# Squares turned and totalled by VectorE, masks added by VectorE, spreads a chunk or more later, gates kept in PSUM, and a launch from a feature-major copy of the input

## The reference

```python
x = x + 0.5 * swiglu(rms_norm(x, g1), w_gate, w_up, w_down)   # width 2816
x = x + mixing(rms_norm(x, g2), ...)
x = x + 0.5 * swiglu(rms_norm(x, g3), ...)
```

## Time and profile before

| | |
|---|---|
| median of 3 runs | 2061.31 us (2059.57 to 2062.02) |
| the profiled execution | 2060.95 us, of which the span from first to last instruction is 2059.0 us |
| TensorE, matmuls | 2031.1 us busy (99% of the span) |
| TensorE, weight loads | 1755.1 us (85%) |
| VectorE | 805.0 us (39%) |
| ScalarE | 1082.1 us (53%) |
| GpSimd | 1575.6 us (77%) |
| transfers | 362.29 MB, 176 GB/s on average |

### The profile page before, as it was taken

The page is one execution under the profiler, slowest core; times in us unless marked ns, Lnnn a source line. Parts: engine busy times, 40 slices in busy tenths (PEclk is TensorE's granted clock), DMA queues, the critical chain, the costliest instruction groups (busy, mean ns, idle before and its releaser), DMA issues.

```text
span 2059.0 us, 35031 instructions
## 1 busy us (share of the span) xinstructions
PE 2031.1 (99%) x12172; PEld 1755.1 (85%) x12172; DVE 805.0 (39%) x1776; ACT 1082.1 (53%) x1879; POOL 1575.6 (77%) x672
## 2 busy tenths in 40 slices
PE   8999999999999999999999999999999999999998
PEld 7888988888888898888888888888888888878887
DVE  3223744222422374422242237632223224763223
ACT  5445545444555554544455457654455445755444
POOL 6888756888888875688888886378887887546886
PEclk9999999999999999999999999999999999999999
DMA  7555534555555553455555554455555555444553
GB/s 251 191 187 184 185 114 130 188 191 186 179 187 192 178 185 113 133 191 186 191 177 188 189 188 135 159 177 188 190 188 180 186 191 177 145 177 156 189 192 125
DMA packets 100977, 362.29 MB, mean 176 GB/s; under 512 B 11808, under 2 KB 13088, under 8 KB 100768
## 3 DMA queue, kind: packets, MB, share of 16 engines
q1 hardware_dynamic: 100320, 359.78, 52.5%
q10 hardware_dynamic: 576, 1.41, 0.2%
HBM read 360.10 MB, written 1.05 MB: 175 GB/s over the span
## 4 chain that ended last, share of the span: by engine, by line
PE 94%; DVE 3%; ACT 1%; DMA 1%; issue 1%; SPq 0%; POOLq 0%; DVEq 0%; POOL 0%; ACTq 0%
PE twin L623 30%; PE twin L629 19%; PE twin L697 9%; PE twin L699 9%; PE twin L698 9%; PE twin L625 4%; PE twin L626 4%; PE twin L813 1%; DMA raw<-in_w_dram 1%; PE twin L670 1%; PE twin L756 1%; PE twin L671 1%; PE twin L672 1%; PE twin L819 1%; DVE early L1702 1%
## 5 line engine op out<-in xcount | busy, mean ns | idle before, releaser
L581 POOL TENSOR_TENSOR wlo<-raw,whi 128x1024 fp32r<-128x1024 f32 (+1 forms) x663 | 1573.7, 2403 | 472.7 <-ACT whi L1313 472.5
L1313 ACT CAST whi<-raw 128x1024 fp32r<-128x1024 f32 x664 | 677.1, 1050 | 75.6 <-PE twin L629 35.9
L1762 DVE TENSOR_TENSOR twin<-twin,mix 128x512 f32<-128x512 f32 x168 | 117.6, 700 | 752.8 <-ACT mix L1372 752.1
L623 PE MATMUL twin<-turned,whi 128*128 128x512 f32 x1344 | 370.0, 396 | 2.4 <-DVE turned L1702 2.1
L623 PE MATMUL twin<-early,whi 128*128 128x512 f32 x1344 | 369.9, 396 | 0.7
L1372 ACT COPY mix<-twin 128x512 f32<-128x512 f32 x168 | 98.6, 587 | 434.6 <-PE twin L629 434.6
L629 PEld LDWEIGHTS twin<-turned,wlo 128*128 128x128 f32 x1936 | 288.1, 190 | 28.9
L629 PE MATMUL twin<-turned,wlo 128*128 128x256 f32 x1936 | 309.2, 282 | 0.0
L699 PE MATMUL twin<-wlo,hhi 128*128 128x512 f32 x720 | 283.7, 394 | 0.0
L697 PE MATMUL twin<-whi,hhi 128*128 128x512 f32 x720 | 283.3, 393 | 0.0
L698 PE MATMUL twin<-whi,hlo 128*128 128x512 f32 x720 | 282.2, 392 | 0.0
(11 more groups left out here) (289 smaller groups left out, 2064.7 us busy)
## 6 DMA issues: line engine op xcount, KB each, us to landing
raw<-in_w_dram SPq DMA_DIRECT2D x680, 512.0 KB, 3.3
con<-in_con_dram ACTq DMA_DIRECT2D x1, 1113.5 KB, 8.5
x<-in_x_dram SPq DMA_DIRECT2D x2, 256.0 KB, 3.8
x<-in_x_dram SPq DMA_DIRECT2D x1, 512.0 KB, 6.0
mix<-in_last_gain_dram SPq DMA_DIRECT2D x1, 512.0 KB, 4.2
out_dram<-xs SPq DMA_DIRECT2D x1, 512.0 KB, 2.6
par<-in_par_dram SPq DMA_DIRECT2D x2, 208.0 KB, 3.3
out_dram<-xs SPq DMA_DIRECT2D x1, 320.0 KB, 2.7
```

The lines of the kernel that those rows point to most:

```text
L581: nc.gpsimd.tensor_tensor(wlo[:, place, cols], raw[:, place, cols], whi[:, place, cols].bitcast(F32), ALU.subtract).then_inc(split_done, 1)
L623: pe.matmul(out, hi, both.rearrange("p c n -> p (c n)"), start=start and k == 0, stop=False, skip_group_check=True)
L1313: nc.scalar.copy(whi[:, place, cols], raw[:, place, cols]).then_inc(hi_done, 1)
L1762: dve.tensor_tensor(both, both, kept[:, s], ALU.add).then_inc(summed, 1)
```

## The change

- **Sums of squares.** `sums` now transposes the squares (four transposes) into a bank, and VectorE's `summed_squares` totals groups of 64 or 128 columns along the free axis. Queries and keys get a bank each (`q_sums`, `k_sums`). ssd has four factors in place of eight, each spread over 128 columns.
- **Masks.** `mask_scores`, `set_masks` and three SBUF tensors go; VectorE adds the mask to two banks at once (`add_mask`), before the maxima of the scores and before ScalarE's exponential of the segments.
- **Stages.** Queries and keys are spread at 19 (before 18), ssd at 25 (24), fox at 27 (26), gla in the middle of 32 (31), sc at 34 (32). VectorE's and ScalarE's parts move with them.
- **Gates.** The exponential stays in PSUM, after ScalarE's copy of the values; VectorE adds and inverts from there for each token half.
- **Launch.** A second input, xt, holds x feature-major. It is loaded into unused columns of `mix` in three parts (two of 256 KiB from ScalarE's queue, 512 KiB from SyncE's), and `thi`, `tlo` are made from it without TensorE. x itself comes later, behind slot 2. Slot 0 is loaded and split by halves, its upper part by GpSimd and its remainder by VectorE, as is slot 1's and half of slot 2's. TensorE runs 15 matmuls of ones by ones at the start, then tiles 0 and 1 by halves, tile 2, the root's spread, tile 3. The squares of x are made after slots 1 and 2 are cast.

The diff, cut:

```diff
-AFTER1 = {9: (("gla_z", 0),), 15: (("xsT", 3), ("qk_sums", 4)), 16: (("rowsT", 2),),
-          17: (("seg0", 0), ("seg1", 1), ("sc0", 7)), 18: (("fox_rq", 2), ("fox_rk", 3)), 19: (("seg2", 0), ("seg3", 1), ("sc1", 4)),
...
+AFTER1 = {9: (("gla_z", 0),), 15: (("xsT", 3), ("q_sums", 4)), 16: (("rowsT", 2), ("k_sums", 1)),
+          17: (("seg0", 0), ("seg1", 1), ("sc0", 7)), 19: (("fox_rq", 2), ("fox_rk", 3), ("seg2", 0), ("seg3", 1), ("sc1", 4)),
...
@@ block.sync
-                    for n in range(RING):
+                    for half in range(2):
+                        cols = slice(half * 512, half * 512 + 512)
+                        sp.dma_start(raw[:, 0, cols], w_d[0, :, cols]).then_inc((s_left, s_raw[0])[half], 16)
+                    for n in range(1, RING):
                         load(L, n)
...
-                        if n == 0:
-                            sp.wait_ge(s_raw[0], 16)
+                        if n == 1:
+                            sp.dma_start(xt[:, 4:8], xt_d[:, 4:8]).then_inc(s_xt[2], 16)
+                        if n == 2:
+                            for T in range(NT):
+                                sp.dma_start(x[:, T, :], x_d[:, T, :]).then_inc(s_x[T], 16)
@@ block.gpsimd
+            for half in range(2):
+                cols = slice(half * 512, half * 512 + 512)
+                pool.wait_ge((s_left, s_raw[0])[half], 16)
+                nc.gpsimd.tensor_copy(whi[:, 0, cols], raw[:, 0, cols]).then_inc(ev("first_hi"), 1)
...
+            pool.wait_ge(hi_done, 3)
+            pool.wait_ge(ev("early_rest"), 5)
+            lower_half(2, 1).then_inc(split_done, 1)
+            pool.wait_ge(hi_done, 4)
+            lower_half(3, 0).then_inc(ev("fourth_rest"), 1)
+            lower_half(3, 1).then_inc(split_done, 1)
@@ block.tensor
+            def first_half_tile(L, n, half):
+                out, first = bank[n], half * (KD // 2)
...
+                for k in range(first, first + KD // 2):
+                    if n == 0:
+                        pe.wait_ge(ev("first_lower"), k + 1)
+                    pe.matmul(out, whi[:, n, k * P:(k + 1) * P], turned[:, k].rearrange("p c n -> p (c n)"), start=k == 0, stop=False, skip_group_check=True)
...
+            def first_steps(L):
...
+                for half in range(2):
+                    for n in range(2):
+                        first_half_tile(L, n, half)
+                for half in range(2):
+                    first_half_tile(L, 2, half)
+                pe.wait_ge(s_con, 16)
+                root_spread(L, 0, ("R", 0))
+                for half in range(2):
+                    first_half_tile(L, 3, half)
...
-                            mm = pe.matmul(out[:, c:c + 2], squares[:, t * SEQ + T * P:t * SEQ + (T + 1) * P], groups, start=(T == 0 and t == 0 and at == 0),
-                                           stop=True, skip_group_check=True)
+                            c = T * SEQ + t * P
+                            mm = pe.transpose(out[:, c:c + P], squares[:, t * SEQ + T * P:t * SEQ + (T + 1) * P], ident)
...
-                    for h in heads:
-                        mask_scores(out[h], maskT[:])
...
-                    for e in range(2):
-                        mask_scores(out[e], maskR[:])
...
+                    return (lambda: branch_spread("gla")) if c == 32 else None
...
+            for _ in range(WARM):
+                pe.matmul(bank[6][:, 0:P], ones[:], ones[:], start=True, stop=True)
@@ block.scalar
+            def first_norm(L):
+                act.sem_inc(hi_done, 1)
+                act.wait_ge(s_gain, 16)
+                for half in range(2):
+                    for k in range(4 * half, 4 * half + 4):
+                        if k % 2 == 0:
+                            act.wait_ge(s_xt[min(k // 2, 2)], 16)
+                        nc.scalar.activation(thi[:, k, :], xt[:, k, :], ACT.Copy, scale=gain_of(L, 0, k)).then_inc(thi_done, 1)
+                    split_hi(L, 1 + half)
+                for T in range(NT):
+                    act.wait_ge(s_x[T], 16)
...
+                split_hi(L, 3)
+                split_hi(L, AHEAD)
...
-                        nc.scalar.activation(m2("gate", 64)[:, T * 32:T * 32 + 24], out[:, GW:GATED], ACT.Exp, scale=-1.0).then_inc(ev("gates_exp"), 1)
-                        drained(L, ("ip", m), nc.scalar.copy(m2("vsw", 512)[:, T * GW:(T + 1) * GW], out[:, 0:GW]))
+                        nc.scalar.copy(m2("vsw", 512)[:, T * GW:(T + 1) * GW], out[:, 0:GW])
+                        nc.scalar.activation(out[:, GW:GATED], out[:, GW:GATED], ACT.Exp, scale=-1.0).then_inc(ev("gates_exp"), 1)
@@ block.vector
+            def first_norm(L, own):
...
+                for k in range(KD):
+                    dve.wait_ge(thi_done, k + 1)
+                    ins = dve.scalar_tensor_tensor(tlo[:, k, :], xt[:, k, :], gain_of(L, 0, k), thi[:, k, :].bitcast(F32), ALU.mult, ALU.subtract)
...
+                    if k == 3:
+                        dve.wait_ge(ev("first_hi"), 1)
+                        lower_first(0, 0)
+                        dve.wait_ge(hi_done, 2)
+                        lower_first(1, 0)
+                dve.wait_ge(ev("first_hi"), 2)
+                lower_first(0, 1)
+                lower_first(1, 1)
+                dve.wait_ge(hi_done, 3)
+                lower_first(2, 0)
+                roots(own, 2 * NT, ev("root_ready"))
...
+            def add_mask(mask):
+                ends = twin[0][:].rearrange("p (h b n) -> p h b n", h=2, b=4)[:, :, 0:3:2, :]
+                return dve.tensor_tensor(ends, ends, bc(mask.unsqueeze(1).unsqueeze(1), [P, 2, 2, P]), ALU.add)
...
+                    own.link(add_mask(c_("negq")))
...
+                def summed_squares(name, sums, n):
+                    wait_full(dve, L, name)
+                    return dve.tensor_reduce(sums, psum(L, name)[:].rearrange("p (g n) -> p g n", g=n), AX, ALU.add)
...
-                        dve.wait_ge(ev("gates_exp"), NT * L.l + NT)
-                        own.link(dve.tensor_scalar(g4[:, :, 0:24], g4[:, :, 0:24], 1.0, None, ALU.add))
-                        own.link(dve.reciprocal(g4[:, :, 0:24], g4[:, :, 0:24]))
+                        for T, m in enumerate((GATES, VSW)):
+                            logits = psum(L, ("ip", m))[:, GW:GATED]
+                            dve.wait_ge(ev("gates_exp"), NT * L.l + T + 1)
+                            own.link(dve.tensor_scalar(logits, logits, 1.0, None, ALU.add))
+                            drained(L, ("ip", m), dve.reciprocal(g4[:, T, 0:24], logits))
+                        wait_drained(dve, L, ("ip", VSW))
```

More of the change, by code:

```diff
@@ L59 @@
 SPARE = 8192
+WARM = 15
 LEFT = 640
@@ L587, in _ @@
                 if begun:
-                    for n in range(1, RING):
+                    for n in range(4, RING):
                         split_lo(L, n)
@@ L798, in ffn @@
                     tail(L, slots, accs, next_norm)
-            def mask_scores(out, mask):
-                ends = bass.AP(out.tensor, out.offset, [out.ap[0], (2 * P, 2), (1, P)])
-                pe.matmul(ends, identR[:], mask.unsqueeze(1).to_broadcast([P, 2, P]), start=True, stop=False, skip_group_check=True)
             half_rows = lambda h: slice(HD * h, HD * h + HD)
@@ L896, in segments @@
                         rows = slice(32 * h, 32 * h + 4)
-                        pe.matmul(out[h][:, 0:SEQ], DL[rows, 0:P], DR[rows, :], start=False, stop=False, skip_group_check=True)
+                        pe.matmul(out[h][:, 0:SEQ], DL[rows, 0:P], DR[rows, :], start=True, stop=False, skip_group_check=True)
                     for h in heads:
@@ L961, in branch_sums @@
                 def branch_sums(b):
-                    out = claim(pe, L, f"{b}_sums")
                     pe.wait_ge(ev(f"{b}_squares"), L.l * (2 if b == "fox" else 1) + (2 if b == "fox" else 1))
                     c = (b in ("fox", "sc")) * 512
-                    full(L, f"{b}_sums", sums(out, m1("sq", 1024)[:, c:c + 512], 0, ones[:, 0:2] if b == "ssd" else c_("half")))
+                    sums(f"{b}_sums", m1("sq", 1024)[:, c:c + 512])
                 def branch_spread(b):
@@ L972, in branch_spread, with keys_and_queries_spread, spread_midway @@
                     full(L, f"{b}_r", spread(out, factors_of(b)))
+                def keys_and_queries_spread():
+                    for i, name in enumerate(("fox_rq", "fox_rk")):
+                        out = claim(pe, L, name)
+                        wait_drained(pe, L, "q_sums")
+                        full(L, name, spread(out, factors_of("qk")[:, i * 512:(i + 1) * 512]))
+                def spread_midway(c):
+                    return (lambda: branch_spread("gla")) if c == 32 else None
                 def keys_turned():
@@ L1058, in first_mixer @@
                         inputs_turned()
-                        out = claim(pe, L, "qk_sums")
                         pe.wait_ge(ev("qk_squares"), L.l * 2 + 1)
```

(3 more changed lines are left out.)

175 lines of the change are left out of this document (100 added, 75 removed).

## The result

The changed kernel takes 2046.7 us (median of 4 runs, 2044.7 to 2047.0) against 2060.4 us (4 runs, 2059.4 to 2062.0): ratio 0.9929, 95% interval 0.9917 to 0.9942. It is 13.8 us faster; forecast were 15.9 less, 2045.4 in a range of 2040.5 to 2052.5. The profiled execution took 2046.69 us around a span of 2044.9.

The account below looks back on a forecast made before the run. TensorE, with work recorded for 99% of the span, was taken as the bound. Launch 3.5, first mixers 10.8 and second mixers 1.6 make 15.9; 2060.95 - 15.9 + 0.36 = 2045.4 us, range 2040.5 to 2052.5.

Parts of the forecast that it names:

- Launch: Start of the kernel: first "down" matmul near 20.9 instead of 24.6, gain 3.7, less 0.2 for a late remainder.
- GpSimd's remainder: Launch: slot 5's remainder, behind two extra half slots, can come a little late; 0.2 us taken off.
- Masks: First mixers: four pairs of mask matmuls leave TensorE, 1.15 us per mixer; VectorE's additions counted at nothing.
- Squares: First mixers: six batches of two-column products become transposes, 0.80 to 0.44 us each; 2.1 us taken per mixer.
- Stalls: First mixers: TensorE's three waits before branch spreads go because the spreads come later, 2.1 us per mixer.
- The last spread: End of the first mixers: scaling, cast and remainder must fit behind the last branch's spread, with 0.4 us of slack.
- the claim of the second segment's bank: First mixers: bank free at 252.4, TensorE wants it 0.7 sooner than 253.46; slack 0.3 us.
- Gates: Second mixers: addition in PSUM shortens the wait for the first pair's probabilities, 0.8 us each, 1.6 for both.
- A: Rival: VectorE becomes late in the first mixers, each losing 3 us in waits; 2051.4 us, chance 0.17.
- D: Rival: the launch keeps TensorE's clock at the lower level, 16 us or more affected; about 2066 us, chance 0.03.
- B: Rival: the launch gains nothing because x arrives at 16.5 instead of 12.9; 2048.9 us, chance 0.10.

Follow-up runs that it names:

- hold: Changed kernel with SyncE issuing slot 1 and all later loads only once the copy's first two parts have landed; 2048.88 us, ratio 0.9937.
- warm30: Changed kernel with 30 instead of 15 warm-up matmuls at the launch; 2045.64 us, ratio 0.9925.
- masks_back: Changed kernel with the masks added by TensorE again and VectorE's mask additions gone; 2048.87 us, ratio 0.9937.
- sums_back: Changed kernel with the squares' sums made by two-column products again instead of transposes; 2052.92 us, ratio 0.9958.
- stages_back: Changed kernel with the four branches' spreads and the work behind them at the earlier stages, new sums kept; 2056.16 us, ratio 0.9972.
- again: Changed kernel measured once more with nothing edited; 2046.79 us, ratio 0.9928.
- gates_back: Changed kernel with the second mixers' old gates: exponential to SBUF ahead of the copy, addition and reciprocal in SBUF; 2050.44 us, ratio 0.9942.
- launch_only: Kernel before the change with only the changed launch added; 2060.63 us against 2060.86, ratio 0.9997.
- states_act: Changed kernel with the 128x768 product of the linear-attention states made by two ScalarE copies instead of VectorE; 2045.72 us, ratio 0.9922.

## Why the prediction was right, and where not

The direction and the size were right, and so was the mechanism of the main part, the first mixers. Step by step:

- **Launch, 3.5 forecast, 0.85 measured** (0.55 to 1.48 over nine profiles). The step that failed is "What comes last is then no longer TensorE but the root", with "TensorE's own side gives nearly the same". The spread is at 20.06 where the terms give about 17.5. One microsecond of that is the root's own: x's last half landed at 13.82, which is what the pace of before gave, and not at 12.9; and ScalarE, busy until 12.93, made four squares in a row, 2.6 us, where I counted two behind x, 1.4. The root itself took 3.0, as forecast, and was ready at 18.46. The other 1.6 are TensorE's: its tiles were what came last. Their first half waited for the second part of the copy until 9.70, which I had not priced at all (5.9 us from issue to landing, with slots and x on the same engines; hold), and the matmuls behind ran at 1.2 GHz for 3.4 us (warm30: 1.24 us in one profile, 0.75 in another). The last 3.4 from spread to "down" were right. GpSimd's remainder was late, as forecast: it held the weight load at 26.44 for 0.39, of which about 0.2 reached the matmuls (24.63 to 27.39 before, 23.46 to 26.44 after).
- **Masks**, 1.15 forecast, 1.26 to 1.29 by masks_back. Right.
- **Squares**, 2.1 forecast, 2.83 by sums_back: the batch replaced was priced right (0.80, measured 0.81 in five of six places and 0.92 in one), the new one too high (0.44, measured 0.35 to 0.36 in five and 0.41 in one).
- **Stalls**, 2.1 forecast. All three are gone, and stages_back shows that they would have become 4.4 us with the new sums. The last spread, where I gave 0.4 of slack, has none of the waits I feared, nor has the claim of the second segment's bank.
- **What I left out of the mixers**: the 0.57 of the new wait. VectorE's busy time in a first mixer rose by 8.1 us (83.07 to 91.21), not by 6, and 1.7 of it is that one product's wait. "Each of them has a chunk of 2.8 us of TensorE in between, so I count the additions at nothing" held for the additions, but the moved stages put line 2108 under GpSimd's instruction. I had that rule beside the gates and did not apply it to VectorE's other products over SBUF. 1.27 + 2.83 + 2.07 - 0.57 = 5.60 against 5.43 measured: the sum of 5.4 was right because two errors met, 0.73 too little for the squares and 0.57 for a wait left out. That is luck.
- **Gates**, 0.8 each forecast; 0.95 at the first pair, by "again" against gates_back, and 0.91 and 0.42 over the whole mixers, whose length differs by up to 1.2 between profiles of the same code. The chain came as told: additions in PSUM take 0.18 and 0.19, and the pair's product in SBUF ends at 1243.68, GpSimd's batch at 1243.66.
- **Feed-forward behind the first mixers**: 0.64 each that no step had. Its cause stays open. Without it the gain would have been 12.5, so the total owes its nearness to this as well: the launch gave 2.65 less than forecast, and 1.28 of that came back from where nothing was changed.

Of the rivals, A (VectorE late in the first mixers) came true in a small form, 0.57 instead of 3 a mixer. D named TensorE's clock: it did fall in the launch, but for 3.4 us and not for the 16 and more that D needed. B was nearer than the forecast for the launch's size (2.65 of the 3.5 missing), with the wrong cause: x was in at 13.82, not at 16.5, and the path did not go through it.

## What to carry to other kernels

Where two chains end within a microsecond of each other, price both from their first transfer on, at the pace that all transfers in flight leave it; "nearly the same" is where a gain is lost. When work is moved from TensorE to VectorE, the stage plan must move with it, and what matters is the whole row of VectorE's work behind the move: look for operations over SBUF alone that slide under a long GpSimd instruction, and give them to ScalarE or put an operand in PSUM. If TensorE must wait for a microsecond or two ahead of full-speed work, matmuls without a use in the gap can keep its clock up; here that was worth 0.4 to 1.2 us.

## What was not expected of the hardware

- The granted clock fell after short idle times: in the launch (idle 0.77 and 1.56 us with 0.8 of matmuls between, then 3.4 us at 1.2 GHz) and in gates_back (1.84 and 1.83 us of idle, 3.4 us each time), while 1.78 and 1.80 in the kernel before, and 1.85 and 1.83 in launch_only, left it up. In the launch, fifteen more matmuls into nothing kept it at 2.4 GHz in both profiles that have them.
- VectorE and GpSimd held each other: 0.96 us became 2.69 for VectorE's product, 2.41 became 2.89 for GpSimd's remainder, and 2.39 again with the product gone (states_act).
- The same feed-forward code takes 186.6 or 187.2 us, with no wait in the trace; the share of transfers and the clock show nothing. That, and the second mixers' 131.9 to 133.2 with the same code (their waits at lines 1242 and 1287 for VectorE come and go), are what differs between profiles of the same code, with the launch's first spread (19.45 to 20.06 in eight).
